# Expert 3's weights in 1 MB pieces, and half of expert 0's down product amid the second gather

## The reference, cut to what matters

```python
def expert_block(args):
    xb, e = args
    return (jax.nn.silu(xb @ w_gate[e]) * (xb @ w_up[e])) @ w_down[e]

ys = lax.map(expert_block, (xs, block_e)).reshape(n_slots, d)
ys = ys * slot_gate[:, None].astype(ys.dtype)
return jax.ops.segment_sum(ys, slot_tok, num_segments=n + 1)[:n]
```

## Time and profile before

| | us |
|---|---|
| median of three runs | 1275.59 |
| time of the profiled execution | 1275.22 |
| its span | 1273.4 |
| PE busy (in the span) | 1186.2 (93%) |
| DVE busy | 453.1 (36%) |
| ACT busy | 179.8 (14%) |
| POOL busy | 70.4 (6%) |
| DMA | 485.58 MB, 381 GB/s over the span |

### The profile page before, as it was taken

One profiled execution on the slowest core, in us unless ns is written; L12 is line 12 of the kernel. 1 busy time (PEld: TensorE's weight loads), 2 busy tenths in 40 slices (PEclk: granted clock), 3 DMA queues, 4 the chain that ended last, 5 costly groups with the idle time before them and its releaser, 6 DMA issues.

```text
span 1273.4 us, 13818 instructions
## 1 busy us (share of the span) xinstructions
PE 1186.2 (93%) x5088; PEld 498.0 (39%) x5088; DVE 453.1 (36%) x952; ACT 179.8 (14%) x381; POOL 70.4 (6%) x87
## 2 busy tenths in 40 slices
PE   7999999899999999999899999999999999988888
PEld 3444445554333333333233376543333333332333
DVE  4297776667211212211211165651122112112122
ACT  2211216632000000000000021410000000000000
POOL 0013100000000000000000000000000000000000
PEclk9899999999999999999999999999999999999999
DMA  9948749479999999999999999799999999999997
GB/s 361 406 168 347 284 176 401 165 290 353 422 421 423 421 423 421 423 421 423 422 422 421 421 395 380 298 378 421 421 423 422 422 422 422 422 422 422 421 421 309
DMA packets 82187, 485.58 MB, mean 381 GB/s; under 512 B 6242, under 2 KB 7906, under 8 KB 32996
## 3 DMA queue, kind: packets, MB, share of 16 engines
q1 hardware_dynamic: 80128, 481.38, 92.6%
q10 hardware_dynamic: 2020, 3.67, 0.8%
HBM read 483.98 MB, written 1.05 MB: 381 GB/s over the span
## 4 chain that ended last, share of the span: by engine, by line
PE 54%; SPq 32%; DMA 5%; DVE 4%; ACT 3%; issue 3%; POOL 0%; ACTq 0%; DVEq 0%; POOLq 0%
SPq L339 25%; PE PS L871 16%; PE PS L667 9%; PE PS L890 8%; SPq L347 5%; PE PS L917 4%; DMA ring<-in_moe_w_down 4%; PE PS L637 2%; PE PS L741 2%; PE PS L1118 2%; PE PS L1094 2%; SPq L353 1%; DVE TMP L1897 1%; PE PS L696 1%; ACT ring L1193 1%
## 5 line engine op out<-in xcount | busy, mean ns | idle before, releaser
L871 PE MATMUL PS<-ring,KQH 128*64 128x512 f32 x2048 | 455.6, 594 | 16.9 <-DMA ring<-in_moe_w_up 15.9
L871 PEld LDWEIGHTS PS<-ring,KQH 128*64 128x64 f32 x2048 | 148.7, 137 | 309.6 <-issue 267.8
L890 PE MATMUL PS<-ring,KQH 128*64 128x512 f32 x960 | 220.9, 602 | 41.0 <-DVE TMP L1897 25.3
L1924 DVE TENSOR_TENSOR KQH<-KQH,PS 128x256 f32<-128x256 f32 x64 | 39.0, 610 | 404.9 <-ACT KQH L1335 404.5
L890 PEld LDWEIGHTS PS<-ring,KQH 128*64 128x64 f32 x960 | 66.6, 137 | 156.5 <-issue 121.2
L917 PE MATMUL PS<-TMP,KQH 128*128 128x512 f32 x256 | 126.4, 617 | 0.2
L1335 ACT ACTIVATE KQH<-PS 128x256 f32<-128x256 f32 x62 | 23.8, 384 | 681.7 <-PE PS L871 672.6
L667 PE MATMUL PS<-ring,KQH 128*128 128x512 f32 x256 | 114.0, 593 | 0.0
L1897 DVE TENSOR_TENSOR TMP<-PS,TMP 64x512 f32<-64x512 f32 x62 | 42.7, 689 | 131.1 <-PE PS L890 105.5
L1897 DVE TENSOR_TENSOR TMP<-PS,KQH 64x512 f32<-64x512 f32 x62 | 42.7, 689 | 127.6 <-PE PS L890 104.0
L498 POOL COPY KQH<-KQH 128x512 f32 x62 | 38.1, 616 | 810.7 <-PE PS L871 761.1
(11 more groups left out here) (261 smaller groups left out, 789.5 us busy)
## 6 DMA issues: line engine op xcount, KB each, us to landing
ring<-in_moe_w_gate SPq DMA_DIRECT2D x128, 1024.0 KB, 25.6
ring<-in_moe_w_up SPq DMA_DIRECT2D x128, 1024.0 KB, 26.3
ring<-in_moe_w_down SPq DMA_DIRECT2D x60, 2048.0 KB, 26.3
ring<-in_ada_w SPq DMA_DIRECT2D x23, 2048.0 KB, 14.6
ring<-in_attn_w_in SPq DMA_DIRECT2D x2, 4096.0 KB, 12.8
ring<-in_moe_w_down SPq DMA_DIRECT2D x8, 1024.0 KB, 27.1
ring<-in_attn_w_in SPq DMA_DIRECT2D x2, 2048.0 KB, 21.4
ring<-in_attn_w_out SPq DMA_DIRECT2D x1, 4096.0 KB, 24.1
```

What stands on the lines that cost most here:

```text
L871: ins = mm(PS[64 * f:64 * f + 64, 4, :], xs[:, k, 0:SLOTS], gu_w[s][:, :, k, 256 * f:256 * f + 256], start=k == 0, stop=k == KC - 1)
L890: ins = mm(PS[64 * f:64 * f + 64, b, :], lhs, dn_w[s][:, c, 512 * f:512 * f + 512], start=c == 0, stop=c == 3)
```

## The change

It acts in both layers, in four places.

- **SP**: expert 3's gate and up weights come in four steps (two DMAs of 0.5 MB each time, k by pairs), its down weights in two DMAs of 1 MB; expert 4's part 0 comes in two steps. The new steps wait for `early_free`, which PE raises after k = 1 and after k = 5 of expert 0's gate and up products, after the first half of expert 0's down product, and after k = 1 of expert 1's. The loop of loads starts at expert 6.
- **PE**: the transposes come after block k = 2 of the second gather instead of k = 3, the first half of expert 0's down product comes after k = 4, and the second half after k = 7. The second gather's blocks use other banks, since bank 6 now holds the down product early.
- **ACT**: the copy to `t_sb` comes before the spread of k = 3.
- **DVE**: both gated outputs of expert 0 are computed between `choose` and `overflow_tiles`, with waits for the gate row and for `dn_done >= 1` ahead of them; `y_sb` is now `KT[:, 1024:2048]`.

```diff
-        y_sb = TMP[:, 0:1024]
+        y_sb = KT[:, 1024:2048]
...
-            b = ((5, 6, 7, 3), (6, 7, 3, 2))[half][k % 4]
+            b = ((5, 6, 7, 3, 5, 6, 7, 3), (6, 7, 3, 2, 7, 3, 2, 7))[half][k]
...
+            def load_fourth(L, s):
+
+                for part in range(2):
+                    for j in range(2):
+                        if j == 0:
+                            sp.wait_ge(early_free, 4 * L.l + part + 1)
+                        else:
+                            sp.wait_ge((L.gu_half, L.gu_done)[part], 1)
+                        k = 4 * part + 2 * j
+                        for a, w in enumerate((w_gate, w_up)):
+                            sp.dma_start(gu_w[s][:, a, k:k + 2, :], w[L.l, 3].rearrange("(p k) f -> p k f", p=P)[:, k:k + 2, :]
+                                         ).then_inc((L.gu_in, L.gu2_in)[part][s] if j else early_in, 16)
+                for a in range(2):
+                    if a == 0:
+                        sp.wait_ge(early_free, 4 * L.l + 3)
+                    else:
+                        sp.wait_ge(L.dn_done, 1)
+                    sp.dma_start(dn_rows[s][:, a], w_down[L.l, 3, 256 * a:256 * a + 256].rearrange("(p b) n -> p b n", b=2)
+                                 ).then_inc(L.dn_in[s] if a else early_in, 16)
...
-                with sp.Fori(0, (NE - 5) // 3) as it:
+                load_fourth(L, L.slot(0))
+                for j in range(2):
+                    if j == 0:
+                        sp.wait_ge(early_free, 4 * L.l + 4)
+                    else:
+                        sp.wait_ge(L.gu_half, 2)
+                    for a, w in enumerate((w_gate, w_up)):
+                        sp.dma_start(gu_w[L.slot(4)][:, a, 2 * j:2 * j + 2, :],
...
+                load_gate_up(L, 4, L.slot(4), True, (1,))
+                load_down(L, 4, L.slot(4), True)
+                load_expert(L, 5, L.slot(5), freed=True)
+                with sp.Fori(1, (NE - 5) // 3) as it:
...
             def gate_up_first(L, e, c, it):
 
+                if c == 3:
+                    pe.wait_ge(early_in, 112 * L.l + 112)
...
-                for k in range(4):
-                    if k == 3:
-                        pe.wait_ge(slots_known, L.l + 1)
+                for k in range(3):
                     second_places(L, k)
                 pe.wait_ge(L.h_ready, 1)
                 transposes(None).then_inc(L.tr_done, 1)
-                for k in range(4, KC):
-                    pe.wait_ge((xs_v, xs_a)[k % 2], (9, 8)[k % 2] * L.l + k // 2 + 3)
-                    second_places(L, k)
+                pe.wait_ge(slots_known, L.l + 1)
+                second_places(L, 3)
+                pe.wait_ge(xs_a, 8 * L.l + 5)
+                second_places(L, 4)
                 pe.wait_ge(L.t_ready, 1)
+                pe.wait_ge(xs_v, 9 * L.l + 5)
+                pe.wait_ge(L.dn_in[L.slot(0)], 16)
+                down_half(L.slot(0), 0, t_sb, 6).then_inc(early_free, 1)
+                pe.wait_ge(xs_v, 9 * L.l + 6)
+                second_places(L, 5)
+                pe.wait_ge(xs_a, 8 * L.l + 6)
+                second_places(L, 6)
                 pe.wait_ge(xs_v, 9 * L.l + 7)
-                pe.wait_ge(L.dn_in[L.slot(0)], 16)
-                down(L.slot(0)).then_inc(L.dn_done, 1)
-                gate_up_first(L, 1, 1, 0)
+                second_places(L, 7)
+                down_half(L.slot(0), 1, t_sb, 6).then_inc(L.dn_done, 1)
+                pe.wait_ge(L.gu_in[L.slot(1)], 32)
+                pe.wait_ge(L.xw_ready, 1)
+                gate_up(L.slot(1), xw[1], range(2)).then_inc(early_free, 1)
+                gate_up(L.slot(1), xw[1], range(2, 4)).then_inc(L.gu_half, 1)
...
-                spread(L, 1, 3)
                 act.wait_ge(L.tr_done, 1)
                 nc.scalar.copy(t_sb[:, 256:512], PS[:, 5, 256:512]).then_inc(L.t_ready, 1)
-                for k in range(5, KC, 2):
+                for k in range(3, KC, 2):
                     spread(L, 1, k)
...
                 choose(PAIR, sg, L.chosen, 1, L.sg_ready)
+                dve.wait_ge(mod_used, TURN[LATE[L.l]] + 1)
+                dve.wait_ge(L.dn_done, 1)
+                for f in range(2):
+                    gated_outputs(L, 0, f).then_inc(L.y_v, 1)
                 overflow_tiles(L)
                 overflow_slots(L)
-                dve.wait_ge(mod_used, TURN[LATE[L.l]] + 1)
...
-                step(0, 0, 0)
+                hidden(2)
```

More of the change, by code:

```diff
@@ L302, in program @@
         end_first = sem("end_first")
+        early_free, early_in = sem("early_free"), sem("early_in")
         end_bank = (7, 5)
@@ L331, in rows_of, with load_gate_up @@
                 return w.rearrange("(k p) n -> p k n", p=P)[:, :, c0:c0 + n]
-            def load_gate_up(L, e, s, freed):
-                for part in range(2):
+            def load_gate_up(L, e, s, freed, parts=range(2)):
+                for part in parts:
                     if freed:
@@ L425, in _ @@
             for L in layers:
-                with sp.Fori(0, (NE - 5) // 3) as it:
+                load_fourth(L, L.slot(0))
[6 more added lines that the diff above has]
+                        sp.dma_start(gu_w[L.slot(4)][:, a, 2 * j:2 * j + 2, :],
+                                     w[L.l, 4].rearrange("(p k) f -> p k f", p=P)[:, 2 * j:2 * j + 2, :]
+                                     ).then_inc(L.gu_in[L.slot(4)] if j else early_in, 16)
+                load_gate_up(L, 4, L.slot(4), True, (1,))
+                load_down(L, 4, L.slot(4), True)
+                load_expert(L, 5, L.slot(5), freed=True)
+                with sp.Fori(1, (NE - 5) // 3) as it:
                     for c in range(3):
@@ L986, in experts @@
                     ins = gate_up(L.slot(0), dense, [k])
+                    if k == 1:
+                        ins.then_inc(early_free, 1)
                 ins.then_inc(L.gu_half, 1)
@@ L997, in experts @@
                     ins = gate_up(L.slot(0), dense, [k])
+                    if k == 5:
+                        ins.then_inc(early_free, 1)
                 ins.then_inc(L.gu_done, 1)
                 pe.wait_ge(picked_in, 4 * L.l + 4)
-                for k in range(4):
-                    if k == 3:
-                        pe.wait_ge(slots_known, L.l + 1)
+                for k in range(3):
                     second_places(L, k)
```

## The result

The changed kernel takes 1278.71 us (median of 8 runs, 1277.29 to 1279.67), the kernel before 1275.17 us in the same comparison: a ratio of 1.0032, 95% interval 1.0022 to 1.0041. It is slower by 3.5 us, where 1276.4 had been forecast with a range to 1280.5. The measured time lies above the range that the forecast's own case had, 1275.4 to 1278.0. The direction is that of the rival in which TensorE's clock falls.

What follows compares the result with a forecast made beforehand. The weight stream's idle time at each layer's expert start bounds the kernel; expert 4's down matrix starting 0.8 us later in layer 0 and 0.0 in layer 1 gives 1276.0, plus 0.37 for the median: 1276.4 us, range 1272.7 to 1280.5.

Steps and rivals of the forecast that it cites:

- the forecast's own case: Both layers' expert starts: earlier pieces' gain is idled away, expert 1's down product is late; 1276.4 us, chance 0.54.
- the rival in which TensorE's clock falls: PE, gap before expert 1's down product: clock halves, 1279.8 us for one layer, 1283.2 for both; chance 0.27.
- The layer ends when its stream ends, and the loss is at its start: Weight DMAs in both layers: only idle time before the stream becomes continuous counts, 5.1 and 6.0 us.
- The floor: PE lets expert 4's down matrix start no earlier than 323.4 us (layer 1: 852.7), 1.2 and 1.7 us before the old start.
- The earlier pieces: SP's loads of expert 3 and expert 4's gate and up: issued earlier, 1.9 us less idle time up to there.
- Its own string: Layer 0's pieces in sequence, 2.49 us each, 1.77 us from issue to full rate; expert 4's gate and up end at 322.7.
- DVE's chain: DVE before expert 1's down product: spread k = 6 1.94 us later, lists' end 3.35, `hidden(2)` 2.08.
- The sum: Expert 4's down matrix starts 0.8 us later in layer 0, 0.0 in layer 1: 1275.22 becomes 1276.0, forecast 1276.4 us.
- The range: Whole kernel, 8 in 10: from the gain, 1272.7, to a clock fall in one layer with some margin, 1280.5 us.
- The argument against the fall: PE before expert 1's down product: full matmuls run to the gap, which is shorter than what the trace's fall followed.
- Small DMAs: SP's twelve 0.5 MB DMAs a layer: priced at zero, though the Trainium skill's fit would give 24 us of fixed time.
- POOL's window, `early_in`: POOL's first window at 308.06 us, PE wants it at 308.3, no stall; the `early_in` wait every sixth expert costs nothing.

Runs made afterwards that it cites:

- Big pieces: Lists last, but experts 3 and 4's gate and up weights in their old 1 MB DMAs; 1274.08 us, ratio 0.9995; again 1273.61 us, 0.9994.
- two halves: Big pieces with expert 4's down matrix in two 1 MB DMAs, the first released by half of expert 1's down product; 1272.87 us, ratio 0.9983.
- Pieces alone: The kernel before with only SP's small pieces, expert 3's down DMAs both waiting for expert 0's whole down product; 1273.93 us, ratio 0.9995.
- gap filled: The changed kernel with two extra full-width products on TensorE behind `add_zero`; 1276.23 us, ratio 1.0010.
- lists last: The changed kernel with the overflow lists behind `hidden(2)` on DVE, waits and count reads behind the expert loops; 1275.04 us, ratio 1.0005.
- DVE's order undone: The changed kernel with DVE's lists first again, then expert 0's first gated output, `hidden(2)`, the second output; 1274.42 us, ratio 1.0003.
- late product: The kernel before with three scratch products on DVE ahead of expert 0's first gated output, two filler products on TensorE; 1279.54 us, ratio 1.0035.

## Why the prediction was right or wrong

- *The layer ends when its stream ends, and the loss is at its start*: right. The ledger orders the kernels nearly as their medians do, though it is above the medians' differences for the gains and for the change.
- *The floor*: right in kind. Big pieces, two halves and the dips between them show that expert 4's down matrix was the next thing to wait for once the stream came earlier.
- *The earlier pieces*: issued as worked out (1.96 us behind the start of the products; 14.04 for the half down matrix, forecast 305.2 less 291.1, so 14.1). The forecast didn't say which of them wins the 1.9 us. Its own string answers it: the fourth piece ends at 305.6, and the half down matrix, issued at 305.2, can start only at 307.0, so the gate and up pieces of expert 3 win nothing. Pieces alone, with the ledger of before, agrees.
- *DVE's chain*: the deciding step held, and was sized too small. Behind the start of the products the spread of k = 6 came 2.04 us later (forecast 1.94), the lists' end 3.75 (3.35), `hidden(2)` and the down product 2.49 (2.08 and 1.96). Of the 0.40 us that the lists' end came later than forecast, 0.31 is the conversion L1920, whose meeting with POOL's copy the forecast didn't look at.
- *The sum*: right in its form, wrong in two of its terms. With the issues of expert 4's down matrix as measured (4.07 and 3.92 us late instead of 1.96 and 1.71) it gives 5.1 us, and the ledger gives 4.9. The clock is the larger term: the forecast took one that stays, and put 0.27 on the fall, though it named the clock of 0.50 as a sign of being wrong. It fell in both layers in both profiles of the change, and cost 1.6 to 1.7 us of product time each (5.24 and 5.35 against 3.65). The rival had taken 3.4, for a whole product at half speed; the fall covered only its first 3 us. The delay is the other term: without the fall (gap filled) the issue is 2.49 and 2.23 us late, and the change costs 1.3 to 1.7 us (ratio 1.0010, medians; ledger 1.5) where 0.8 was forecast.
- *The range*: that it holds the measured time is partly luck. The rival's own price for what happened, a fall in both layers, was 1283.2 us, outside the range to 1280.5; the time lies inside because each fall cost half of what had been taken.
- *The argument against the fall*, that the gap was shorter than what the earlier fall followed, did not hold. And that the trace of before has one fall was a misreading: it has another at 649 to 652.5 us (the window above), under the same down product. Its rows would have given the price, 5.35 us for the product, and a gap of only 0.88 us ahead of it:

```profile
645.68 1.87 PE L703 MATMUL PS<-KQH,cols 128*128 128x32 f32 x16
...
648.89 5.35 PE L890 MATMUL PS<-ring,KQH 128*64 128x512 f32 x16 [0.88 <-DVE TMP L1897]
```

- *Small DMAs*: at nothing, as forecast, in pieces alone; the lists last leave room for up to 0.9 us in layer 1. The estimate of 24 us by the Trainium skill's fit counted all twelve DMAs of 0.5 MB, though they stand in place of six of 1 MB: only six are additional, 12 us by the same fit.
- *POOL's window, `early_in`*: at nothing, as forecast. POOL had the first window at 307.40 (306.82 and half of 1.16), PE wanted it at 307.68.

Open: why the clock falls at one gap and not at a nearly equal one, and why the medians differ by less than the ledger (3.5 for 4.9, 1.5 for 2.4).

## What to carry to other kernels

When loads go through one queue in order, add up the idle time of the stream and find the load that sets its next floor; earlier pieces ahead of it win nothing until that one moves. Work placed ahead of a link of a chain on an in-order engine counts in full, and so does what the moved work waits for: here half a product on PE delayed a list on DVE that an activation on ACT waited for. A gap that grows by 2 us on TensorE is to be priced with its clock, and a filler of idle products tells that share apart at once.

## What the runs showed of the hardware

- TensorE's clock fell to 0.50 behind a gap of 2.45 us with four short transposes and another 0.87 us behind it, full matmuls before and after; two products of filler, which left 0.73 and 0.87 us idle, kept it at 1.00. In the late product the same filler left 1.64 and 0.87 us idle, and the clock fell (its PE):

```profile
319.01 0.43 PE L879 MATMUL PS<-const,KQH 128*128 128x128 f32 x2 [1.64 <-DVE KQH L1925]
...
320.53 5.01 PE L890 MATMUL PS<-ring,KQH 128*64 128x512 f32 x16 [0.87 <-DVE TMP L1898]
```

- The length of the gap doesn't sort the cases cleanly. With DVE's order undone PE idled 1.31 and 0.87 us in layer 0, without a filler, and the clock stayed at 1.00; in layer 1 of the late product it idled 1.37 and 0.95 us, and the clock fell. At 649 us of the kernel before it fell behind sixteen products of 32 columns, the transposes and 0.88 us of idle.
- The fall near 649 us comes in some profiles and not in others, and costs nothing there. The change has it in its first profile and not in its second, with 987.5 us from the start of the products to the end in both; the kernel before has it (982.3 us), pieces alone hasn't (982.5).
- DVE's conversion of 128x7 elements in the lists took 0.46 to 0.48 us in the six places where POOL's copy of 128x512 ran at the same time (both profiles of the change and gap filled, both layers), and 0.17 us in the six where it didn't (before, DVE's order undone and pieces alone).
- The DMAs of 0.5 MB (36292 packets under 8 KB in the page, 32996 before) took nothing from the stream where it waited for something else anyway (pieces alone: the ledger equal within 0.1 us), in spite of their number.
